# The residual stream of a two-block layer kept token by token: rows scaled on VectorE, TensorE only transposes

## The reference

```
h = h + rms_norm(concat(attn, conv) @ w_out, mix_post_g)        # attn, conv from rms_norm(h, mix_pre_g) @ w_in
hn = rms_norm(h, ffn_pre_g)
h = h + rms_norm((silu(hn @ w_gate) * (hn @ w_up)) @ w_down, ffn_post_g)    # d_ff = 2816
xn = rms_norm(h, norm1_g)                                       # second block: gated mixing, top-k attention
h = h + merged @ w_o
xn = rms_norm(h, norm2_g)
h = h + peer(xn)                                                # 8 heads pick 16 experts each of 128 x 128
```

## Time and profile before

| | |
|---|---|
| runs | 2374.46 us median of 3 (2373.32 to 2376.76) |
| profiled execution | 2374.6 us, span 2372.9 us |
| TensorE | busy 2231.6 us (94%), mean granted clock 0.968 |
| VectorE, ScalarE, GpSimd | 62%, 38%, 36% |
| DMA | 458.21 MB, 193 GB/s over the span |

### The profile page before, as it was taken

The page is one execution under the profiler, slowest core; times in us unless marked ns, Lnnn a source line. Parts: engine busy times, 40 slices in busy tenths (PEclk is TensorE's granted clock), DMA queues, the critical chain, the costliest instruction groups (busy, mean ns, idle before and its releaser), DMA issues.

```text
span 2372.9 us, 28906 instructions
## 1 busy us (share of the span) xinstructions
PE 2231.6 (94%) x10687; PEld 1883.8 (79%) x10687; DVE 1481.2 (62%) x2602; ACT 891.4 (38%) x1306; POOL 850.8 (36%) x458
## 2 busy tenths in 40 slices
PE   6987799999959889998999999999998999999999
PEld 4855478888837666777999999999997888888777
DVE  4972411110052784324687999999956888888887
ACT  4353332222234434234433445555532333333332
POOL 1102144444313223334466632222234444333442
PEclk8998899999979999999999999999999999999999
DMA  3301133333222222223444479999999999999996
GB/s 135 98 10 44 45 89 98 95 99 93 87 58 73 70 63 67 84 89 104 129 138 134 150 243 300 305 288 299 300 356 330 378 390 381 376 375 370 360 368 250
DMA packets 253432, 458.21 MB, mean 193 GB/s; under 512 B 116428, under 2 KB 165485, under 8 KB 253165
## 3 DMA queue, kind: packets, MB, share of 16 engines
q1 hardware_dynamic: 118028, 296.98, 36.9%
q0 software_dynamic: 36864, 134.23, 15.6%
q10 hardware_dynamic: 98400, 25.17, 4.7%
HBM read 404.28 MB, written 52.04 MB: 192 GB/s over the span
## 4 chain that ended last, share of the span: by engine, by line
PE 72%; DVE 10%; issue 8%; DMA 5%; ACT 3%; POOL 2%; SPq 1%; another core or an unknown queue 0%; DVEq 0%; POOLq 0%; ACTq 0%
PE bank L423 22%; PE bank L427 21%; PE bank L426 21%; PE bank L820 4%; DMA wraw<-in_peer_v 3%; DMA wraw<-in_peer_u 2%; POOL WL L985 2%; DVE cacc L1502 1%; PE bank L460 1%; ACT WH L1017 1%; DVE m L1709 1%; PE bank L790 1%; PE bank L525 1%; ACT sc L1085 0%
## 5 line engine op out<-in xcount | busy, mean ns | idle before, releaser
L423 PE MATMUL bank<-XH,WH 128*128 128x384 f32 (+2 forms) x1992 | 745.4, 374 | 64.3 <-DVE XL L1456 13.1
L985 POOL TENSOR_TENSOR WL<-wraw,WH 128x1024 fp32r<-128x1024 f32 (+1 forms) x190 | 489.6, 2589 | 845.7 <-ACT WH L1017 845.6
L427 PE MATMUL bank<-XH,WL 128*128 128x384 f32 (+2 forms) x1992 | 729.1, 366 | 0.0
L426 PE MATMUL bank<-XL,WH 128*128 128x384 f32 (+2 forms) x1992 | 729.0, 366 | 0.0
L1017 ACT ACTIVATE WH<-wraw 128x1024 fp32r<-128x1024 f32 (+1 forms) x413 | 433.5, 1055 | 489.4 <-DMA wraw<-in_peer_v 213.3
L423 PEld LDWEIGHTS bank<-XH,WH 128*128 128x128 f32 (+1 forms) x1992 | 380.7, 191 | 118.2 <-issue 59.4
L426 PEld LDWEIGHTS bank<-XL,WH 128*128 128x128 f32 (+1 forms) x1992 | 381.3, 191 | 40.1 <-issue 2.2
L427 PEld LDWEIGHTS bank<-XH,WL 128*128 128x128 f32 (+1 forms) x1992 | 379.8, 191 | 40.6
L1992 DVE TENSOR_TENSOR WL<-wraw,WH 128x1024 fp32r<-128x1024 f32 x223 | 273.0, 1224 | 130.6 <-ACT WH L1017 130.1
L996 POOL DMA_INDIRECT hT<-in_peer_u_rows,gidx x128 | 178.0, 1391 | 374.1 <-DVE gdot L2003 357.3
L423 PE MATMUL bank<-WH,GH 128*128 128x512 f32 x768 | 303.9, 396 | 0.8 <-DVE GL L2058 0.8
(11 more groups left out here) (288 smaller groups left out, 2417.8 us busy)
## 6 DMA issues: line engine op xcount, KB each, us to landing
wraw<-in_peer_u SPq DMA_DIRECT2D x128, 512.0 KB, 5.1
wraw<-in_peer_v SPq DMA_DIRECT2D x128, 512.0 KB, 8.1
gate_matrices<-Gs ACTq DMA_DIRECT2D x6, 4096.0 KB, 37.7
gr<-gate_matrices SPq DMA_DIRECT2D x128, 192.0 KB, 6.7
activations<-ac SPq DMA_DIRECT2D x118, 192.0 KB, 4.1
ar<-activations SPq DMA_DIRECT2D x118, 192.0 KB, 5.0
wraw<-in_w_gate SPq DMA_DIRECT2D x22, 512.0 KB, 3.8
wraw<-in_w_up SPq DMA_DIRECT2D x22, 512.0 KB, 3.6
```

Of the source, the lines that this page charges most:

```text
L423: mm = pe.matmul(out, wh, xh, start=first, stop=False)
L426: pe.matmul(out, wh, xl, start=False, stop=False)
L427: return pe.matmul(out, wl, xh, start=False, stop=last)
L985: pool.tensor_tensor(WL[:, u % NW, 0:m], wraw[:, u % NR, 0:m], WH[:, u % NW, 0:m].bitcast(F32), ALU.subtract).then_inc(s("w_lo"), 1)
```

## The change

The residual stream is now `hN` [128 tokens, 4 tiles, 1024], token by token.

- **Norms.** ScalarE squares a row tile with an accumulator (`norm_root`), so the sum of squares is one number per partition, and takes its root; VectorE inverts [128, 1] and scales the tile to `yN` (`scale_rows`). TensorE transposes it (`turned`: four transposes to a bank, 16 a half of the tokens); ScalarE reads the bank times the gain to `XH` (`high_half`), VectorE to `XL` (`low_half`). The sums by `ones` are gone, but for the conv layer norm.
- **Halves.** The first two or three units after norms 0, 1 and 3 work on 256 tokens at a time (`by_halves`); `ci` has an order of its own.
- **Branches.** `wo`, `wd` and `wo2` are computed token by token (`rows_of`): the activations are stationary and 512 columns of weights move. Their last two units go tile by tile (`rows_tail`), so that row tiles end one after another. Branch squares, roots, gain and addition follow per tile (`row_square`, `row_root`, `gained`, `add_rows`); the gain lies in `gain_row`, loaded by SyncE.
- **Order.** Two of the eight `wo` units stand before `pw`, beside the layer norm of the conv. `brow` stands behind the first three projections. `turn_back` is gone. Casts go up to three units ahead at the norms. The gathered expert rows lie in `y`, where `hT` was used before. Unit ci+2 is streamed before `second_inputs`.

Core of the diff:

```diff
+            def by_halves(n, keys):
+                outs = {}
+                def part(i, half):
+                    unit_key, key = keys[i]
+                    if half == 0:
+                        outs[i] = take(*key)
+                    wh, wl = unit_views(unit_key)
+                    tok = half_of_tokens(half)
+                    for k in range(KD):
+                        if k % 2 == 0:
+                            wait_read(pe, ("xt", n, half, k // 2))
+                        mm = split(outs[i][:, tok], wh[:, k, :], wl[:, k, :], XH[:, k, tok], XL[:, k, tok], k == 0,
+                                   k == KD - 1, begins=k == 0 and half == min(i, 1))
+                    if half == 1:
+                        full(mm, *key)
+                turned(n, 0)
+                for i in range(len(keys)):
+                    part(i, 0)
+                    if i == 1:
+                        turned(n, 1)
+                for i in range(len(keys)):
+                    part(i, 1)
...
             def prepare():
-                square_sum(0)
...
             def first_projections():
+                by_halves(0, [(key, key) for key in (("cg", 0), ("ca", 0), ("cg", 1))])
+                bias_rows()
...
             def feed_forward():
-                for c in range(KF):
-                    tile(("wg", c), ("fg", c), ready=("x_lo", KD) if c == 0 else None)
+                by_halves(1, [(("wg", 0), ("fg", 0)), (("wu", 0), ("fu", 0)), (("wg", 1), ("fg", 1))])
+                tile(("wu", 1), ("fu", 1))
+                for c in range(2, KF):
+                    tile(("wg", c), ("fg", c))
                     tile(("wu", c), ("fu", c))
...
+            def rows_and_norm(name, j, last, gain):          # ScalarE
+                n = j + 1
+                if j < 2:
+                    cast_to((name, 0, last))
+                    for t in range(NT):
+                        row_square(j, 0, t)
+                cast_to((name, 1, last))
+                for t in range(NT):
+                    if j < 2:
+                        row_square(j, 1, t)
+                        row_root(j, t)
+                    if t:
+                        norm_root(n, t - 1)
+                cast_to((name, 1, last), 2)
+                high_half(n, 0, gain, range(KD // 2))
+                norm_root(n, NT - 1)
+                high_half(n, 0, gain, range(KD // 2, KD))
+                cast_to((name, 1, last), 3)
+                high_half(n, 1, gain)
...
+            def scale_rows(n, t):                            # VectorE
+                dve.wait_ge(s("norm_roots"), n * NT + t + 1)
+                link(dve.reciprocal(h_rec[:, t:t + 1], h_root[:, t:t + 1]))
+                dve.tensor_scalar(yN[:, t, :], hN[:, t, :], h_rec[:, t:t + 1], None, ALU.mult).then_inc(s("rows_scaled"), 1)
...
+                if name == "ci":                             # TensorE
+                    turned(2, 0)
+                    outs = [take(name, t) for t in tiles_of(0)]
+                    part(0, tiles_of(0))
+                    part(1, tiles_of(0), False)
+                    turned(2, 1)
+                    outs += [take(name, t) for t in tiles_of(1)]
+                    part(2, tiles_of(0), False)
+                    part(0, tiles_of(1), False)
+                    part(1, tiles_of(1))
+                    part(2, tiles_of(1))
+                    part(3, range(NT))
```

More of the change, by code:

```diff
@@ L450, in tile, with square_sum @@
                 full(project(unit_key, out[:, 0:tokens], tokens=tokens, **kw), *key)
[L452 to L462, removed]
-                    mm.then_inc(s("squares_used"), 1)
-                else:
-                    full(mm, "ss", m)
+            def square_sum():
+                for k in range(CC):
+                    pe.wait_ge(s("squares"), k + 1)
+                    mm = pe.matmul(bank_of(("ss", 1))[:, :], ones[:, :], sq[:, k % RING, :], start=k == 0,
+                                   stop=k == CC - 1)
+                    if k < CC - 1:
+                        mm.then_inc(s("squares_used"), 1)
+                    else:
+                        full(mm, "ss", 1)
@@ L597, in feed_forward @@
-                add_square(4, KD - 1)
-                square_sum(5)
-            def turn_back(i):
-                t, half = i // 2, i % 2
-                out = take("hn", i)
-                for k in range(4):
-                    mm = pe.transpose(out[:, k * P:(k + 1) * P], hT[:, half * 4 + k, t * P:(t + 1) * P], ident[:, :])
-                full(mm, "hn", i)
-            def natural(name, between):
+                rows_of("wd", ("rows", 1), fH, fL, KF // 2 - 1, ready=lambda k: pe.wait_ge(s("f_lo"), k + 1))
@@ L846, in _ @@
             attention()
[L847 to L848 removed]
+            mix = []
+            conv_tail(mix)
+            mix_out(mix)
             feed_forward()
@@ L1426, in _ @@
             merge_and_out()
+            rows_and_norm("wo2", 2, 3, "norm2")
             choose_experts()
@@ new lines, in low_half @@
+            def low_half(n, half, gain, chunks=range(KD)):
+                tok = half_of_tokens(half)
+                for c in chunks:
+                    dve.wait_ge(s("x_hi"), (2 * n + half) * KD + c // 2 * 2 + 2)
+                    src = wait_full(dve, ("xt", n, half, c // 2))
+                    at = c % 2 * HALF
+                    made = dve.scalar_tensor_tensor(out=XL[:, c, tok], in0=src[:, at:at + HALF], scalar=vcol(gain, c),
+                                                    in1=XH[:, c, tok].bitcast(F32), op0=ALU.mult, op1=ALU.subtract)
+                    if c % 2:
+                        made.then_inc(frees(("xt", n, half, c // 2)), 1)
```

452 lines of the change are left out of this document (255 added, 197 removed).

## The result

The changed kernel takes 2293.55 us in the median (2290.35 to 2300.09, 4 runs), the kernel before 2374.1 beside it: ratio 0.966, 95% interval 0.964 to 0.969. Five more runs of it in the experiments (e0_again) gave 2291.78 (2290.73 to 2295.2).

The account below looks back on a forecast made before the run. TensorE, busy 94% of the span, was taken as the bound, with gains sought where it idles or does sums. 13.0 + 3.8 + 10.9 + 21.3 + 20.7 + 12.8 - 2 = 80.5; 2374.6 - 80.5 = 2294 us, range 2278 to 2314.

Parts of the forecast that it names:

- Sums off TensorE, norm 1: Seven sum steps each leave `wo` and `wd`, gaining 13.0 us; norm 1's drain after `wo` gains 21.3.
- lag: From the last matmul before a norm to when following units would run without gap; norm 1: 34.3 to 13.0 us.
- the rival of a slow narrow matmul: 256-column matmuls after norms fall to 0.45 us each, costing 127 us more: 2421; chance 0.03.
- Norm 2: Drain between `wd` and `ci`: GpSimd's mask of `spatial_w` ends last, first `ci` matmul at 16.5 us; gain 20.7.
- Norm 3 and `turn_back`: Drain after `wo2` shortens to a lag of 9.0, gaining 12.8 us; 32 `turn_back` transposes dropped gain 3.8.
- Start: Three units done at 44.5, then `brow` 6 us, delaying `skew_rows` and conv taps; loss 2 us, bounds +4 and -6.
- the stall of unit 6: At the start, unit 6 lands 6.5 us later, so VectorE's low half comes near 68 instead of 65.56.
- Conv tail: Two `wo` units fill TensorE's 9.03 us idle before `pw`, which starts near 197.5 as before; gain 10.9 us.
- `wo` 16 to 19 us sooner after attention: Sign the forecast was right: moved units and seven dropped sum steps end `wo` 17.4 us sooner relative to attention.
- It survives: the last stage has TensorE busy throughout: The whole 80.5 us gain reaches the run's end, TensorE being busy 548.2 of 552 us in the last stage.

Follow-up runs that it names:

- e0_again: The changed kernel itself, unedited, run five more times beside the edits; 2291.78 us.
- e3: Changed kernel with GpSimd masking `spatial_w` ahead of unit ci+3 instead of ahead of `ci`; 2288.94 us.
- e1: Changed kernel with ScalarE's casts of units 1 and 2 at the start moved ahead of the first and second high halves; 2283.47 us.
- e2: Changed kernel with `brow` ahead of the first transposes, its table loaded and spread first, VectorE copying instead of ScalarE; 2294.44 us.
- e5: Changed kernel with ScalarE's cast of `pw`'s second unit behind the four high halves of the conv output instead of ahead; 2285.48 us.
- e9: Changed kernel with an unused tile of 4 columns where `nst` was; 2301.14 us.
- e8: Kernel before the change with tile `nst` 16 columns wide instead of 4; 2373.7 us.
- e11: Kernel before the change with tile `nst` 32 columns wide (128 bytes a partition); 2373.2 us.
- e4: Changed kernel with the two `wo` units listed, cast and run behind `pw`, as before the change; 2299.66 us.

## Why the prediction was right, and where it was not

The time was right (2293.55 for 2294). Part by part:

- **Sums off TensorE, norm 1** (6.5 of 13.0, and 21.3): 27.2 measured for 27.8. The lag is 12.6 us (371.6 less 66 units of 5.44) for 13.0. On VectorE there is one collision in the drain, as was assumed. The 256-wide matmuls start 0.12 us apart as taken, so the rival of a slow narrow matmul is out. The Trainium skill (TensorE: Matmul & The Clock Gate, Back-to-back issue gap) lists 262 cycles for 256 columns, 109 ns; these rows show some 10 ns more, and they decide.
- **Norm 2** (20.7): 21.8. That GpSimd's mask bounds it, e3 shows. ("5 parts of 2.7 to 36.7" should read four: from 25.8, five would end at 39.3. The sum had used 36.7.)
- **Norm 3 and `turn_back`** (16.6): 15.3.
- **Start** (loss of 2): attention 3.2 later (4.9 in the kernels with most matmuls at the half clock), and `cmean` 4.6 later. The step behind the number failed. The prediction let the loss come from "SyncE sends `skew_rows` out at 51", the stall of unit 6 and the conv taps queued behind it. The stall came as forecast (low half at 67.77 for 68), but costs nothing: e1 keeps it and moves attention by 10.4, and e2, without it, gains nothing in TensorE's row but the clock. What counts is TensorE's row, full up to attention: three units 3.6 us earlier, but `brow`'s 5.6 more in that row, and the stretch behind it 1.2 longer (six matmuls at the half clock). "I get the three units done at 44.5" was 3.6 early as well: unit 2 was ready at 33.9 (31.9 forecast) and its 24 matmuls then ran at the half clock.
- **Conv tail** ("`pw` can start near 197.5 as before"): the step that cost most. From `cmean` to the end of `wo` the change gains 10.7 us (87.7 to 77.0) where 10.9 and 6.5 were forecast, and the sign that was to show the prediction right, `wo` 16 to 19 us sooner after attention, failed: 9.3. The words "two casts are now among ScalarE's work there, 1 us each" count them on ScalarE alone, but GpSimd's low half behind one of them stands over VectorE's subtractions. e5 gives 4.0 to 6.5 us back by moving it. The wait of 1.71 us for banks was in no term, nor was a clock of 0.79 and 0.92 over `pw` and `wo`. The two units brought 6.1 to 8.8 instead of 10.9.
- **"It survives: the last stage has TensorE busy throughout"**: it did survive, but the stage was taken as unable to change. It became 1 to 13 us shorter (6.2 in the table), with matmuls 3% closer together. That the placement of tiles sets this distance in the changed kernel, e9 shows; that it is also what the change altered is likely, but e8 and e11 failed to bring it about in the kernel before. With the slow distance, by e9, the run would be 2301, 7 over the forecast and still inside its range.

So the mechanism was right for the sums and the three norms and wrong for the start and the conv tail, and that the total is exact is luck: an error of 9 us ahead of norm 1 (1.2 up to attention, 1.4 in attention, 6.7 behind it) was made up by 9 elsewhere, 6 of them of a cause that the prediction didn't know and 3 within the scatter.

## What to carry to other kernels

Before a stall on one engine is costed, read the busy share of the others in the stretch up to the next meeting point: here TensorE was full, so VectorE's stall of 5.7 us was free, and `brow`'s 5.6 us moved into that stretch cost their full time. Where two engines are nearly full, as here before the change (58.4 and 57.3 of 59 us), the shares don't say which decides; an edit that frees one and keeps the other's stall, like e1, does. Count the matmuls at the half clock in both profiles before a gain of a few us is credited to an edit. When a cast is moved, follow it to the engine that works on it next: where GpSimd's low half lands on VectorE is part of the move. And a stage that a change doesn't touch may change its pace with the placement of tiles: compare the distance of equal matmuls before and after, ahead of crediting the gain to the change.

## What the runs showed of the hardware

- Most of TensorE's matmuls of 512 columns in the last stage start 0.2267 or 0.2333 us apart at a granted clock of 1.00, with the same operands, depending on an unused tile of 16 bytes a partition (e9).
- After a wait of 3.61 us ahead of `pw` the granted clock was 0.79 in the mean of the next 17.5 us, with 14 matmuls at the half level (1.2 GHz); after one of 0.94 us it was 1.00 over 14.6 (e5). The clock cost 2.9 us there, as much as the wait. The length of the wait alone doesn't set it: after 3.60 us in e1 six matmuls ran at the half level, and after 11.8 us in e4 seven.
- VectorE's low half with one input from a bank is spared by GpSimd's (0.40 us each, e1). A scaling of one SBUF tile (2.76 us beside GpSimd's low half, 0.75 without) and a subtraction of two (four take 4.23 us beside it, 2.50 without) are not.
